# Two-layer diffusion backbone on one core: expert rows turned at the arm's end, results turned in pairs of units, arms at block heads

## The chip, the cores and the metric

One core of a Trainium2 chip runs the whole program. The metric is the device time of one execution in microseconds. The program uses the core's engines: TensorE (PE, matmuls and transposes), VectorE (DVE), ScalarE (ACT), GpSimd (POOL, here issuing DMAs and filling with zeros) and SyncE (SP, issuing the stream of weights). All data are float32; a float32 matmul is two matmul records in the trace, a transpose one.

## What is computed

A latent sequence of 256 tokens, width 1024, goes through two layers. Layer 0 is a mixer (attention and Fourier groups) and a dense SwiGLU. Layer 1 is a gated short convolution and then a mixture of experts, where the change is:

```python
def moe_swiglu(h, router, w_gate, w_up, w_down):
    probs = jax.nn.softmax((h @ router).astype(jnp.float32), axis=-1)
    vals, idx = lax.top_k(probs, TOP_K)                      # 2 of 8 experts per token
    wts = vals / jnp.sum(vals, axis=-1, keepdims=True)
    combine = jnp.sum(jax.nn.one_hot(idx, N_EXPERTS) * wts[..., None], axis=-2)
    out = jnp.zeros_like(h)
    for e in range(N_EXPERTS):
        out = out + combine[..., e:e + 1] * swiglu(h, w_gate[e], w_up[e], w_down[e])
    return out
```

Each expert has gate and up weights of 1024 x 3584 and down weights of 3584 x 1024, 44 MB together. Only the tokens that chose an expert are computed by it.

## The kernel before

**The stream of weights.** All weights lie in one tensor in the order of use and are read in units of 2 MB into a ring of seven slots (`ring`). SyncE issues them in this order (L254); each waits until TensorE has handed its slot back (`used`). An expert has 14 gate/up units (`GU_UNITS`) and 7 down units.

**Arms.** How many tokens an expert has is known only at run time. For each of seven widths (64, 96, 128, 144, 160, 192, 256 token rows) TensorE has a code of its own, an arm: L1341 and what follows, once per width. Behind each arm stands a chain of compare-and-branch instructions (`enter_arm`, L1199 to L1201) that jumps to the arm of the next expert. The other engines run one loop over the eight experts. In this run the widths are 64, 96, 144, 64, 128, 64, 96, 64.

**Gate and up.** In the narrow arms (64 and 96) the tokens' rows hTe are the stationary side and the ring's weights move (L1256); the product has tokens on the partitions. ScalarE takes the silu (L456), VectorE multiplies (L804) into aT. Since down needs channels on the partitions, the result of each unit is transposed: `turn` (L1226) is issued for unit u-1 behind the matmuls of unit u, into PSUM bank 6 or 7 by u's parity, and ScalarE's `take_turned` (L449) copies the whole bank of 512 columns back into aT. The last unit is turned inside the first down unit. For 32-row parts (in arm 96) two units share one transpose. In the wide arms (128 and up) the weights are the stationary side (L1238) and nothing has to be turned.

**Down and combine.** Seven down units (L1301) accumulate in banks 4 to 7; behind the last of them the result y is copied to SBUF, half by ScalarE (L475) and half by VectorE (L812), both waiting for `ye_ps`. `combine` (L1327) waits for both copies (`ye_act`, `ye_dve`), multiplies y by the weighted selection selT, and VectorE adds the four results to y_sum (L816). Combine's first matmul hands the last down unit's slot back.

**The next expert's rows.** The rows routed to each expert lie in DRAM; GpSimd reads the 1 MB of an expert into xn (L310) as soon as TensorE has transposed the expert before it (`gather_ps`). `turn_expert` (L1174) transposes xn into banks 0 to 3 in 16 transposes; it waits for xn and for all gate/up products of the present expert. `take_gather` modulates the result into hTe, four pieces of 128x256 on ScalarE (L435) and four on VectorE (L784). `turn_expert` is called in `down` behind unit `TURN_AFTER` = 3. On ScalarE and VectorE, `take_gather` stands between the expert's gate/up work and its copies of y.

An arm begins by waiting for hTe (`hTe_act`, `hTe_dve`).

Of the kernel before, what the change touches and what calls it, by code (L numbers as in the profile page):

```python
# [21 lines left out]
P = 128  # L22
# [22 lines left out]
PART = 256  # L45
WIDTHS = (64, 96, 128, 144, 160, 192, 256)
WIDE = 2
TURN_AFTER = 3


BLOCKS = {64: [(0, 64)], 96: [(0, 64), (64, 32)], 128: [(0, 128)], 144: [(0, 128), (128, 32)],
# [47 lines left out]
def build(nc, stream, x_in, ctx_in, vecs, consts, rope, dft, gains, ada_b, norm_w, late, out):  # L99
    ctx = ExitStack()  # L100
    with ctx:
# [213 lines left out]
        def _(act):  # L315
# [127 lines left out]
            with act.Fori(0, E) as e:  # L443
                act.reg_alu(which, widths, 7, ALU.bitwise_and)
                act.reg_alu(widths, widths, 3, ALU.logical_shift_right)

                def take_turned(u):
                    act.wait_ge(eT_ps, e * GU_UNITS + u + 1)
                    act.activation(aT_e[:, u, :, :].rearrange("p b n -> p (b n)"), ps[:, 6 + u % 2, :],  # L449
                                   ACT.Copy).then_inc(eT_ok, 1)  # L450

                def silu_units(wide):
                    for u in range(GU_UNITS):
                        act.wait_ge(e_ps, e * GU_UNITS + u + 1)
                        q = 2 * (u % 2)
                        act.activation(gated_e[:, u % 2, :, :], ps[:, q:q + 2, 0:SEQ], ACT.Silu).then_inc(e_silu, 1)  # L456
                        if u and not wide:
                            take_turned(u - 1)
                        if u == 5:
                            act.wait_ge(selT_ps, e + 1)  # L460
                            act.activation(selT[:, :, :].rearrange("p b t -> p (b t)"), ps[:, 4, :],
                                           ACT.Copy).then_inc(selT_ok, 1)
                    if wide:
                        act.sem_inc(eT_ok, GU_UNITS)
                    else:
                        take_turned(GU_UNITS - 1)

                with act.If_lt(which, WIDE):
                    silu_units(False)
                with act.Else():  # L470
                    silu_units(True)
                take_gather(e * 4 + 4)
                for b in (1, 0):
                    act.wait_ge(ye_ps, e * 4 + 4 - 2 * b)
                    act.activation(y_slot[:, b, 0:BANK], ps[:, 4 + 2 * b, :], ACT.Copy).then_inc(ye_act, 1)  # L475
# [353 lines left out]
        def _(pe):  # L829
# [365 lines left out]
            def enter_arm(name):  # L1195


                for i, width in enumerate(WIDTHS[:-1]):
                    pe.br_eq(which, i, on_true=f"arm{width}", on_false=f"{name}_not{width}")  # L1199
                    nc.switch_bb(f"{name}_not{width}")  # L1200
                pe.br(f"arm{WIDTHS[-1]}")  # L1201

            def is_wide(width):
                return WIDTHS.index(width) >= WIDE
# [9 lines left out]
                    return [] if u % 2 else [u - 2, u - 1] if u else []  # L1214
                return [u - 1] if u else []

            def turn(e, width, u):

                pe.wait_ge(e_a, e * GU_UNITS + u + 1)
                if u >= 2:  # L1220
                    pe.wait_ge(eT_ok, e * GU_UNITS + u - 1)
                for b, (s0, n) in enumerate(BLOCKS[width]):
                    if n == 32 and u % 2 == 0:
                        continue
                    for c in range(2 if n == P else 1):
                        last = pe.transpose(ps[:, 6 + u % 2, b * 256 + c * P:b * 256 + (c + 1) * P],  # L1226
                                            aT_e[:, u, b, c * P:(c + 1) * P], ident)
                last.then_inc(eT_ps, 1)

            def gate_up(e, width):  # L1230
                for u in range(GU_UNITS):
                    landed_of(e, u)
                    if u >= 2:
                        pe.wait_ge(e_a, e * GU_UNITS + u - 1)
                    done, count = done_before(width, u), 0
                    for b, g, k in wide_steps(width):
                        w = ring[:, (BASE + u) % RING, k * 512 + g * 256 + b * P:k * 512 + g * 256 + (b + 1) * P]
                        last = pe.matmul(ps[:, 2 * (u % 2) + b, g * SEQ:g * SEQ + width], w, hTe[:, k, 0:width],  # L1238
                                         start=(k == 0), stop=(k == KD - 1))
                        if count < len(done):  # L1240
                            last.then_inc(used[(BASE + done[count]) % RING], 1)
                        count += 1
                    for b, (s0, n) in enumerate([] if is_wide(width) else BLOCKS[width]):
                        tiles = P // n
                        if tiles == 4 and u % 2 == 0:
                            continue
                        bank = 2 * (u % 2) + b
                        for k in range(KD):
                            for r in range(tiles):
                                v = u if tiles < 4 else u - 1 + r // 2  # L1250
                                w = ring[:, (BASE + v) % RING, k * 512:(k + 1) * 512]
                                to = ps[n * r:n * (r + 1), bank, :]
                                if tiles > 1:
                                    w = w.rearrange("p (g c n) -> p g c n", g=2, c=2)[:, :, r % 2, :]
                                    to = to.rearrange("p (g c n) -> p g c n", g=2, c=2)[:, :, 0, :]
                                last = pe.matmul(to, hTe[:, k, s0:s0 + n], w, start=(k == 0), stop=(k == KD - 1))  # L1256
                                if count < len(done):
                                    last.then_inc(used[(BASE + done[count]) % RING], 1)
                                count += 1
                    last.then_inc(e_ps, 1)  # L1260
                    if u == 1:
                        pe.wait_ge(comb_ok, e * 4 + 4)
                    if u and not is_wide(width):
                        turn(e, width, u - 1)
                    if u == 5:

                        pe.wait_ge(selw_ok, e + 1)
                        for b, (s0, n) in enumerate(BLOCKS[width]):
                            for t in range(TB):
                                for r in range(P // n):  # L1270
                                    last = pe.matmul(ps[n * r:n * (r + 1), 4, b * SEQ + t * P:b * SEQ + (t + 1) * P],
                                                     selw[:, t, s0:s0 + n], ident, start=True, stop=True)
                        last.then_inc(selT_ps, 1)

            def down(e, width):
# [4 lines left out]
                for d in range(NFE // 4):  # L1280
# [5 lines left out]
                    for b, (s0, n) in (blocks[::-1] if d == final else blocks):  # L1286
# [22 lines left out]
                        if d < final and b == len(blocks) - 1:  # L1309
                            last.then_inc(used[s], 1)  # L1310
                        if d == 0 and b == 0 and not is_wide(width):
                            turn(e, width, GU_UNITS - 1)
                    if d == TURN_AFTER:
                        turn_expert(e)
                if is_wide(width):
# [135 lines left out]
```

## Time and profile before

| | us |
|---|---|
| median of 3 runs | 1543.69 (1540.67 to 1544.56) |
| profiled execution | 1544.38 |
| its span | 1542.5 |
| TensorE busy in it | 1462.2 (95%) |
| chain that ended last: TensorE, DMA, VectorE, issue | 84%, 9%, 4%, 2% |
| transposes of gate/up results (L1226) | 98 |
| ScalarE evictions of them (L449) | 84, 49.9 busy |
| transposes of the experts' rows (L1174) | 128 |

The expert part runs from 578.8 us to the end. TensorE is busy nearly throughout, but the experts of arm 64 end with TensorE waiting for landings of the ring. "Issue" in the chain is time in which an engine waited for nothing that the profile shows. Ends of matmuls are modelled. PEclk is the granted clock of TensorE, 1.00 for 2.4 GHz and 0.50 for 1.2 GHz.

### The profile page before, as it was taken

The numbers are of one execution on the slowest core, as the hardware profiler recorded it, in microseconds if no ns is written. First come the engines' busy times: TensorE is split into PE (matmuls) and PEld (weight loads), VectorE is DVE, ScalarE is ACT, GpSimd is POOL, SyncE is SP. The second block draws the span as 40 slices with busy tenths as digits, with TensorE's granted clock in tenths as the row PEclk, the third lists the DMA queues.
The fourth block names the chain that finished last, engine by engine and source line by source line (L and its number), as shares of the span: only waits on it lengthen the run. The fifth ranks groups of instructions, "written<-read, shape, count | busy, mean of one in ns | idle before, by whom it ended". The sixth has DMA issues, their size and how long they took to land.

```text
span 1542.5 us, 21924 instructions
## 1 busy us (share of the span) xinstructions
PE 1462.2 (95%) x9456; PEld 936.5 (61%) x9456; DVE 378.1 (25%) x658; ACT 257.9 (17%) x501; POOL 28.5 (2%) x32
## 2 busy tenths in 40 slices
PE   5999999999999969989989999998999999999897
PEld 2445498884488556445449984454997464553452
DVE  2659512330047432111010100111010111110112
ACT  3236210000110022211110000121010121121122
POOL 1000002000000001000000000000000000000000
PEclk8899999999999979999999999999999999999999
DMA  9864267971659539999987776799978899999895
GB/s 384 343 240 184 106 275 285 423 274 55 218 203 369 223 109 370 429 425 425 427 351 273 254 259 257 280 428 425 426 294 307 308 404 425 428 427 425 366 428 243
DMA packets 39023, 492.71 MB, mean 319 GB/s; under 512 B 4032, under 2 KB 4320, under 8 KB 10512
## 3 DMA queue, kind: packets, MB, share of 16 engines
q1 hardware_dynamic: 32800, 467.90, 75.1%
q0 software_dynamic: 5840, 22.26, 3.8%
q8 instruction: 88, 1.44, 0.4%
q10 hardware_dynamic: 288, 1.05, 0.2%
q14 instruction: 7, 0.06, 0.0%
HBM read 479.66 MB, written 11.53 MB: 318 GB/s over the span
## 4 chain that ended last, share of the span: by engine, by line
PE 84%; DMA 9%; DVE 4%; issue 2%; ACT 1%; SPq 0%; DVEq 0%
PE ps L1256 21%; PE ps L1301 15%; PE ps L1238 14%; PE ps L1040 10%; DMA ring<-stream 9%; PE ps L1017 9%; PE ps L1091 5%; PE ps L886 4%; PE ps L1226 1%; PE ps L1327 1%; DVE acc L547 1%; DVE att L610 1%; PE ps L1163 1%; PE ps L1174 1%; PE ps L988 0%
## 5 line engine op out<-in xcount | busy, mean ns | idle before, releaser
L1256 PE MATMUL ps<-ring,hTe 128*64 128x256 f32 (+1 forms) x3584 | 359.4, 382 | 7.6 <-issue 3.7
L1301 PE MATMUL ps<-ring,aT 128*64 128x512 f32 (+2 forms) x1232 | 287.0, 597 | 10.2 <-DMA ring<-stream 8.8
L1256 PEld LDWEIGHTS ps<-ring,hTe 128*64 128x64 f32 (+1 forms) x3584 | 215.2, 130 | 129.6 <-issue 16.9
L1238 PE MATMUL ps<-hTe,ring 128*128 128x144 f32 (+1 forms) x1792 | 214.7, 284 | 8.5 <-issue 8.5
L1238 PEld LDWEIGHTS ps<-hTe,ring 128*128 128x128 f32 x1792 | 214.0, 194 | 10.3 <-issue 10.3
L1301 PEld LDWEIGHTS ps<-ring,aT 128*64 128x64 f32 (+2 forms) x1232 | 96.9, 139 | 184.1 <-issue 174.8
L804 DVE TENSOR_TENSOR aT<-hT,ps 128x512 f32<-128x512 f32 x112 | 77.0, 688 | 526.1 <-ACT hT L456 526.1
L456 ACT ACTIVATE hT<-ps 128x512 f32<-128x512 f32 x112 | 66.9, 597 | 522.4 <-PE ps L1256 312.2
L1040 PE MATMUL ps<-hT,ring 128*128 128x256 f32 (+1 forms) x832 | 153.4, 347 | 0.0
L1040 PEld LDWEIGHTS ps<-hT,ring 128*128 128x128 f32 x832 | 138.1, 191 | 15.7 <-issue 1.0
L547 DVE SCALAR_TENSOR_TENSOR acc<-ring,silu_c,acc 128x1024 f32<-128x1024 f32 (+1 forms) x92 | 105.2, 1143 | 2.1 <-DVE acc L547 0.2
L1017 PE MATMUL ps<-ring,aT 128*128 128x512 f32 x240 | 104.5, 594 | 0.0
L1091 PE MATMUL ps<-hT,ring 128*128 128x256 f32 (+1 forms) x480 | 83.9, 337 | 0.0
L1091 PEld LDWEIGHTS ps<-hT,ring 128*128 128x128 f32 x480 | 76.2, 191 | 7.9 <-issue 0.5
L1017 PEld LDWEIGHTS ps<-ring,aT 128*128 128x128 f32 x240 | 45.1, 190 | 56.2 <-issue 56.2
L784 DVE TENSOR_SCALAR hTe<-ps,ab 128x256 f32<-128x256 f32 x36 | 17.2, 537 | 179.6 <-PE ps L1174 171.7
L449 ACT ACTIVATE aT<-ps 128x512 f32<-128x512 f32 x84 | 49.9, 594 | 18.2 <-PE ps L1226 18.2
L886 PE MATMUL ps<-ring,hT 128*128 128x512 f32 x96 | 43.1, 610 | 1.3 <-DVE hT L534 1.3
L435 ACT ACTIVATE hTe<-ps,ab 128x256 f32<-128x256 f32 x36 | 17.5, 563 | 154.9 <-PE ps L1174 145.7
L1226 PEld LDWEIGHTS ps<-cst,aT 128*128 128x128 f32 x98 | 12.5, 139 | 35.2 <-issue 35.2
L886 PEld LDWEIGHTS ps<-ring,hT 128*128 128x128 f32 x96 | 18.8, 197 | 24.7 <-issue 23.7
L812 DVE COPY acc<-ps 128x512 f32<-128x512 f32 x16 | 10.7, 689 | 84.5 <-PEq L1285 61.7
(190 smaller groups left out, 708.5 us busy)
## 6 DMA issues: line engine op xcount, KB each, us to landing
ring<-stream SPq DMA_DIRECT2D x222, 2048.0 KB, 13.5
rows_of_experts<-aT POOLq DMA_DIRECT2D x1, 8192.0 KB, 60.2
xn<-rows_of_experts POOLq DMA_DIRECT2D x8, 1024.0 KB, 17.0
gg<-norm_w POOLq DMA_DIRECT2D x4, 512.0 KB, 14.7
x<-x_in SPq DMA_DIRECT2D x1, 1024.0 KB, 5.1
hTe<-ctx_in SPq DMA_DIRECT2D x1, 1024.0 KB, 7.9
out<-x ACTq DMA_DIRECT2D x2, 512.0 KB, 2.7
aT<-dft POOLq DMA_DIRECT2D x1, 512.0 KB, 11.1
```

What stands on the lines that cost most here:

```text
L449: act.activation(aT_e[:, u, :, :].rearrange("p b n -> p (b n)"), ps[:, 6 + u % 2, :], ACT.Copy).then_inc(eT_ok, 1)
L456: act.activation(gated_e[:, u % 2, :, :], ps[:, q:q + 2, 0:SEQ], ACT.Silu).then_inc(e_silu, 1)
L547: last = dve.scalar_tensor_tensor(out=dst, in0=slot(what)[:, k * D:(k + 1) * D][:, cols], scalar=silu_c[:, 4 * h + k, 0:1], in1=dst, op0=A ...
L804: dve.tensor_tensor(aT_e[:, u, :, :], gated_e[:, u % 2, :, :], ps[:, q:q + 2, SEQ:2 * SEQ], ALU.mult).then_inc(e_a, 1)
L886: last = pe.matmul(ps[:, blk, :], lhs[:, k, b * P:(b + 1) * P], w[:, k, :], start=(k == 0), stop=(k == KD - 1))
L1017: last = pe.matmul(ps[:, 4 + 2 * b + h, :], lhs(k)[:, b * P:(b + 1) * P], w[:, k % per_unit, h * BANK:(h + 1) * BANK], start=(k == 0), sto ...
L1040: last = pe.matmul(ps[:, j % 4, g * SEQ + t0:g * SEQ + t1], w[:, j % 2, g, k, :], hT[:, k, t0:t1], start=(k == 0), stop=(k == KD - 1))
L1091: last = pe.matmul(ps[:, bank, c + t0:c + t1], w[:, i % 4, k, :], hT[:, k, t0:t1], start=(k == 0), stop=(k == KD - 1))
L1226: last = pe.transpose(ps[:, 6 + u % 2, b * 256 + c * P:b * 256 + (c + 1) * P], aT_e[:, u, b, c * P:(c + 1) * P], ident)
L1238: last = pe.matmul(ps[:, 2 * (u % 2) + b, g * SEQ:g * SEQ + width], w, hTe[:, k, 0:width], start=(k == 0), stop=(k == KD - 1))
L1256: last = pe.matmul(to, hTe[:, k, s0:s0 + n], w, start=(k == 0), stop=(k == KD - 1))
L1301: last = pe.matmul(ps[n * r:n * (r + 1), 4 + bank, :], a_T, w[:, f, half * BANK:(half + 1) * BANK], start=(j < max(1, tiles // 2)), stop=( ...
```

## The change

Three edits. `TURN_AFTER` goes from 3 to 6, the last down unit. `turn` takes a pair of units and is issued behind every even unit from 2 on, and once inside the first down unit; a pair's transposes lie in one bank, 128 columns for each unit and block, and one eviction takes them. Ahead of the last branch in each `enter_arm` stands an instruction that aligns addresses, so that the next arm begins at the head of a block of 256 instructions.

```diff
-TURN_AFTER = 3
+TURN_AFTER = NFE // 4 - 1
...
-                def take_turned(u):
-                    act.wait_ge(eT_ps, e * GU_UNITS + u + 1)
-                    act.activation(aT_e[:, u, :, :].rearrange("p b n -> p (b n)"), ps[:, 6 + u % 2, :],
-                                   ACT.Copy).then_inc(eT_ok, 1)
+                def take_turned(pair):
+                    act.wait_ge(eT_ps, e * GU_UNITS + 2 * pair + 2)
+                    act.activation(aT_e[:, 2 * pair:2 * pair + 2, :, 0:P],
+                                   ps[:, 6 + pair % 2, :].rearrange("p (u b n) -> p u b n", u=2, b=2),
+                                   ACT.Copy).then_inc(eT_ok, 2)
...
-                        if u and not wide:
-                            take_turned(u - 1)
+                        if u and u % 2 == 0 and not wide:
+                            take_turned(u // 2 - 1)
...
+                pe.addr_align(256, offset=255, max_nops=0)
                 pe.br(f"arm{WIDTHS[-1]}")
...
-            def turn(e, width, u):
+            def turn(e, width, pair):
 
-                pe.wait_ge(e_a, e * GU_UNITS + u + 1)
-                if u >= 2:
-                    pe.wait_ge(eT_ok, e * GU_UNITS + u - 1)
-                for b, (s0, n) in enumerate(BLOCKS[width]):
-                    if n == 32 and u % 2 == 0:
-                        continue
-                    for c in range(2 if n == P else 1):
-                        last = pe.transpose(ps[:, 6 + u % 2, b * 256 + c * P:b * 256 + (c + 1) * P],
-                                            aT_e[:, u, b, c * P:(c + 1) * P], ident)
-                last.then_inc(eT_ps, 1)
+                pe.wait_ge(e_a, e * GU_UNITS + 2 * pair + 2)
+                if pair >= 2:
+                    pe.wait_ge(eT_ok, e * GU_UNITS + 2 * pair - 2)
+                for u in range(2):
+                    for b, (s0, n) in enumerate(BLOCKS[width]):
+                        if n == 32 and u == 0:
+                            continue
+                        last = pe.transpose(ps[:, 6 + pair % 2, u * 256 + b * P:u * 256 + (b + 1) * P],
+                                            aT_e[:, 2 * pair + u, b, 0:P], ident)
+                last.then_inc(eT_ps, 2)
...
-                    if u and not is_wide(width):
-                        turn(e, width, u - 1)
+                    if u and u % 2 == 0 and not is_wide(width):
+                        turn(e, width, u // 2 - 1)
...
-                            turn(e, width, GU_UNITS - 1)
+                            turn(e, width, GU_UNITS // 2 - 1)
```

TensorE's order at the end of arm 64, from the first down unit to the chain of branches, before (L1226 turns the last unit, L1301 is down, L1174 the next expert's rows, L1327 combine; a count is that of matmuls in the program):

```order
L1301 MATMUL ps<-ring,aT 64x512 x8
L1219 REGISTER_ALU
L1226 MATMUL ps<-cst,aT 128x128
L1301 MATMUL ps<-ring,aT 64x512 x8
L1180 REGISTER_ALU
L1301 MATMUL ps<-ring,aT 64x512 x16
L1169 ISA
L1174 MATMUL ps<-cst,xn 128x128 x16
L1301 MATMUL ps<-ring,aT 64x512 x24
L1320 ISA
L1327 MATMUL ps<-acc 128x512 x4
```

and in the changed kernel, where the same lines are L1303, L1228, L1175 and L1329:

```order
L1303 MATMUL ps<-ring,aT 64x512 x8
L1221 REGISTER_ALU
L1228 MATMUL ps<-cst,aT 128x128 x2
L1303 MATMUL ps<-ring,aT 64x512 x8
L1181 REGISTER_ALU
L1303 MATMUL ps<-ring,aT 64x512 x40
L1170 ISA
L1175 MATMUL ps<-cst,xn 128x128 x16
L1322 ISA
L1329 MATMUL ps<-acc 128x512 x4
L1350 REGISTER_ALU
```

The 16 transposes of the next expert's rows now stand between the last down matmul and combine.

VectorE's order at the end of each expert, in the changed kernel (L785 modulates the gathered rows, L813 copies y, L817 adds the combined results); but for the line numbers the order is that of before:

```order
L785 TENSOR_SCALAR hTe<-ps,ab 128x256 x2
L784 REGISTER_ALU
L785 TENSOR_SCALAR hTe<-ps,ab 128x256 x2
L812 REGISTER_ALU
L813 COPY acc<-ps 128x512
L812 REGISTER_ALU
L813 COPY acc<-ps 128x512
L817 TENSOR_TENSOR acc<-acc,ps 128x512
```

Nothing moved on VectorE: its copies of y stand behind the modulated copies in both programs.

## Rows read from the trace of the kernel before

**Rows 1.** Chain that ended last, in order of time: start us, us, what

```profile
796.70 3.33 issue
...
1068.08 5.14 issue
1073.22 45.36 PE ps L1238 x384
...
1119.03 57.17 PE ps L1238 x512
...
1443.63 3.41 issue
```

**Rows 2.** Timeline, end of e3: start us, us, engine, line, operation, count [idle before <-releaser]

```profile
1051.39 1.97 PE L1174 MATMUL ps<-cst,xn 128*128 128x128 f32 x16
1052.08 1.93 ACT L435 ACTIVATE hTe<-ps,ab 128x256 f32<-128x256 f32 x4 [10.44 <-PE ps L1174]
1052.96 1.90 DVE L784 TENSOR_SCALAR hTe<-ps,ab 128x256 f32<-128x256 f32 x4 [14.69 <-PE ps L1174]
...
1053.28 7.09 PE L1301 MATMUL ps<-ring,aT 128*64 128x512 f32 x32
...
1061.73 1.29 DVE L812 COPY acc<-ps 128x512 f32<-128x512 f32 x2 [6.88 <-PEq L1285]
1061.76 3.65 PE L1301 MATMUL ps<-ring,aT 128*64 128x512 f32 x16 [1.38 <-DMA ring<-stream]
...
1066.10 1.99 PE L1327 MATMUL ps<-acc 64*128 64x512 f32 x8 [0.69 <-ACT acc L475]
```

**Rows 3.** Timeline of TensorE in e1 (arm 96), transposes between gate/up units

```profile
681.29 0.33 PE L1226 MATMUL ps<-cst,aT 128*128 128x128 f32 x1
681.55 3.67 PE L1256 MATMUL ps<-ring,hTe 128*64 128x256 f32 x32
685.16 0.44 PE L1226 MATMUL ps<-cst,aT 128*128 128x128 f32 x2
685.53 4.68 PE L1256 MATMUL ps<-ring,hTe 128*64 128x256 f32 x48
```

**Rows 4.** Timeline of TensorE from e0 to e1, then from e5 to e6

```profile
663.09 3.65 PE L1301 MATMUL ps<-ring,aT 128*64 128x512 f32 x16 [2.60 <-DMA ring<-stream]
...
669.35 3.67 PE L1256 MATMUL ps<-ring,hTe 128*64 128x256 f32 x32
674.10 7.26 PE L1256 MATMUL ps<-ring,hTe 128*64 128x256 f32 x96 [1.07 <-DMA ring<-stream]
...
1309.58 3.65 PE L1301 MATMUL ps<-ring,aT 128*64 128x512 f32 x16 [1.29 <-DMA ring<-stream]
...
1321.03 1.30 PE L1256 MATMUL ps<-ring,hTe 128*64 128x256 f32 x10 [1.52 <-DMA ring<-stream]
```

**Rows 5.** Stretches, while the next arm's code is due: us, engines, PEclk, DMA share, GB/s

```profile
1227.00:1229.50 2.50, 2.50 (x7) 1.06 (x7) 0.77 (x2) 1.00 (x1) 0.00 (x0) 1.00 0.40 85
1444.00:1446.00 2.00, 0.00 (x0) 0.00 (x0) 1.30 (x3) 0.00 (x0) 0.00 (x0) 1.00 0.99 410
```

**Rows 6.** Timeline of TensorE: near the start, from e4 to e5, head of e7

```profile
23.01 3.48 PE L864 MATMUL ps<-ring,silu_c 128*2 128x512 f32 x16 [2.94 <-DMA ring<-stream]
...
1226.71 3.70 PE L1327 MATMUL ps<-acc 128*128 128x512 f32 x8 [0.69 <-ACT acc L475]
1230.67 7.34 PE L1256 MATMUL ps<-ring,hTe 128*64 128x256 f32 x64 [0.27 <-issue]
...
1447.04 8.54 PE L1256 MATMUL ps<-ring,hTe 128*64 128x256 f32 x64 [3.41 <-issue]
```

**Rows 7.** Stretches behind three idle times; the columns of rows 5

```profile
23.00:26.00 3.00, 2.99 (x16) 0.44 (x16) 0.00 (x0) 0.00 (x0) 0.00 (x0) 0.53 1.00 425
661.00:665.00 4.00, 1.91 (x10) 0.92 (x12) 1.29 (x2) 0.60 (x1) 0.00 (x0) 1.00 1.03 432
...
1446.60:1449.90 3.30, 2.86 (x14) 1.76 (x16) 0.00 (x0) 0.00 (x0) 0.00 (x0) 0.50 0.73 313
```

More of the change, by code:

```diff
@@ L465, in silu_units @@
                     else:
-                        take_turned(GU_UNITS - 1)
+                        take_turned(GU_UNITS // 2 - 1)
                 with act.If_lt(which, WIDE):
```

## The prediction

> **What bounds the kernel now.** I read the chain that ended last first, in order of time [rows 1]. In the expert part (from 578.8 us on) it consists of TensorE matmuls, broken by landings of weight units and by three pieces called issue: 3.33, 5.14 and 3.41 us in which TensorE has no work between two experts. The eight experts need arms 64, 96, 144, 64, 128, 64, 96, 64; I call them e0 to e7. An arm-64 expert works through a gate/up unit in 3.87 us (3.61 in [rows 3] and 0.26 for a transpose), while a 2 MB unit at the 432 GB/s of [rows 7] takes 4.9 us: e0, e3 and e5 catch up with the stream and end waiting for it [rows 2, 4]. e1, e2, e4, e6 and e7 are bound by TensorE. A delay of an expert's start also delays the slots it hands back, so it passes on in full even through e3 and e5; only TensorE work inside the waiting stretch of e0, e3 and e5 is free.
>
> **1. The rows move behind the last down unit.** The 16 transposes take 1.89 us of TensorE wherever they stand (1051.39 to 1053.28 in [rows 2]). What hangs on them does not. ScalarE and VectorE execute in program order, and in both programs their four modulated copies of the gathered rows stand ahead of their copies of the down result; combine waits for the latter. Before, the modulated copies ran under the last three down units: ScalarE started 0.69 and VectorE 1.57 us after the transposes' start, VectorE was busy for 1.90 us, and nobody noticed. At the expert's end the down copies were ready, and combine began 0.69 us after the last down matmul (1065.41 to 1066.10).
>
> In the new place the same sequence starts at the last down matmul's end: VectorE begins at 1.57, is done at 3.47, then makes its two down copies, 1.29 us (1061.73 in [rows 2]), to 4.78; combine starts at about 4.8. ScalarE starts 0.9 earlier, also with four modulated and two down copies, and is not the last. So combine comes 4.8 instead of 0.7 after the last down matmul, 4.1 later, less the 1.9 that no longer stand between the units: **+2.2 us** where TensorE is the bound. For wide arms I take the same: there too combine began 0.69 after the last down matmul [rows 6], and VectorE's two copies, of which one used to lie under the last unit, now both come late. Five places are of this kind: e1 to e2, e2 to e3, e4 to e5, e6 to e7, and the end of e7, whose transposes serve nobody but are issued: 5 x 2.2 = 11.0.
>
> Behind a stream-bound expert the 1.9 are no gain, since they lay in its wait, but something else is: the 1 MB reload of xn that the transposes release moves out of the way of the last units. It costs the ring half a unit's time, 2.4 us, and I put half of that, 1.3, before the last down unit's landing and all of it before the landing of the next expert's second unit.
> - e3 to e4: 4.1 - 1.3 = 2.8, in round terms **+2.7**.
> - e0 to e1: last down starts 663.1 - 1.3, ends 3.65 later, combine 4.8 after that, the arm 1.9 after combine: 672.1; its second unit starts 3.6 later at 675.7 against 674.10 now, which was set by a landing [rows 4]: **+1.6**.
> - e5 to e6 likewise: 1309.6 - 1.3 + 3.65 + 4.8 + 1.9 + 3.6 = 1322.2 against 1321.03: **+1.2**.
>
> Together 16.5. The ring slot that combine's first matmul hands back also comes 4.1 later, but behind e2 and e4 the unit loaded into it is needed only six units on, and behind the others five or more slots are already queued: nothing.
>
> **2. Pairs.** In [rows 3] one transpose costs 0.26 us from its start to the next gate/up matmul, two in a row 0.37; so the first costs 0.26 and each further one 0.11. A pair of units cost 0.26 + 0.26 in arm 64 and costs 0.37; in arm 96 it cost 0.26 + 0.37 and costs 0.48: 0.15 less, seven times an expert, 1.05. Three narrow experts are bound by TensorE (e1, e6, e7): **-3.2**. In e0, e3 and e5 it vanishes in the wait for the stream. ScalarE saves seven of fourteen evictions, but it idles between units. The pair's later eviction holds nobody: the down units wait for theirs in the same order, and the last pair is turned inside the first down unit, as the last unit was.
>
> **3. Arms at block heads.** I take the three stalls as the fetch of the next arm's code, since TensorE waits there for nothing that the profile shows; from combine's start (1066.10 in [rows 2]) to the arm's (1073.22 in [rows 1]) it is 7.1 us. Would a block head shorten it? [rows 6] speaks against it: arm 64 was entered at the same instruction from e4 and from e6, once 3.96 us after combine's start with 0.27 of idle time, once with 3.41 idle. What differs is the load on the DMA engines that have to bring the code: share 0.40 behind e4, where no stall is seen, 0.99 behind e6, where one is [rows 5]. The code waits behind weight units, wherever in a block it starts. Between 0 and all three stalls (11.9 us) I take **0**.
>
> The Trainium skill, Runtime: NRT & Kernel Launch, section Instruction fetch mechanics, has it that a taken branch to a block outside the two that are present must wait for the fetch. It says nothing about the place within a block, and by it a jump into the next block, which arm 96 behind arm 64 now becomes, stays free: by the page this edit is worth 0.
>
> **4. TensorE's clock.** The move makes a new idle stretch of 4.8 - 1.9 = 2.9 us at each of eight ends. The idle stretch of 3.41 us ahead of e7 was followed by half clock, 1.2 GHz (0.50 granted in the 3.3 us from 1446.6), one of 2.94 near the start as well (0.53 in the 3 us behind it); one of 2.60, ended at 663.09, was not (1.00) [rows 4, 6, 7]. 2.9 lies between. The price: e4's first 384 matmuls took 45.36 us where 57.17/512 gives 42.9, 2.5 too many [rows 1]; e7's first 64 took 8.54 against e5's 7.34, 1.2 [rows 6]. Behind e1, e3 and e6 a slow combine hides in the wait for the code, and the arm's head ran at half clock already: nothing new. In the other five places (ends of e0, e2, e4, e5, e7) a fall costs about 1.5 us, as combine and the next matmuls run slow. Bounds 0 and 5 x 1.7 = 8.5; since the nearest row (2.94) fell and the next one below did not, I take three of five: **+4.5**.
>
> **Sum.** 16.5 - 3.2 + 0 + 4.5 = +17.8 on the profiled execution's 1544.4 us (span 1542.5 and 1.9 around it) is 1562.2; the median shown, 1543.7, is 0.7 lower: **1561.5 us**, 1.2% slower. With the clock term at its ends and 1 to 2 us of doubt in the stream-bound places, this case reaches from 1554 to 1568.
>
> **Rivals.**
> - *Block heads pay (the other side).* If the fetch of an arm that starts inside a block is what takes 7.1 us, because the little that is left of the block runs out and a second fetch is awaited, then all three stalls go (11.9), and with them the half clock behind them (2.5, 1.2, and 1.8 taken for e2, between them: 5.5): 13.3 - 17.4 = -4.1, 1539.6; each fall of the clock from term 4 adds 1.5. It wins as soon as the heads give more than the 13 to 18 us of the other terms. For it: the stalls are real and the largest idle pieces. Against it: [rows 5, 6]. 10%.
> - *The late jump finds the stream drained.* Combine now comes some 3 us later behind e1 and e6, and the transfers were near their end there: 0.73 share right behind e7's start [rows 7]. If the code is then fetched as fast as behind e4, each arm starts up to 3.3 us earlier and warm: 2 x (3.3 + 1.5) = 9.6 less, 1552. 9%.
> - *Arm 96 loses its free entry.* Behind arm 64 it followed directly in the program and was entered without a stall (at 669.35 in [rows 4], where its combine had just ended). Now padding lies between, and its block may have to be fetched: 7.1 - 1.9 = 5.2 us twice, and half clock behind each: about 1573. 8%.
> - Something else, such as copies that overlap more than I assume: 3%.
>
> **How the numbers follow.** The forecast's case has 70%. The range leaves out the first rival and the upper half of the third: 1549 to 1571. A measurement of this kernel can tell about 0.3%, 4.6 us, from no change. The first rival lies at that bound, 1540 with no fall of the clock and up to 1546 with some: I split it with half of the rest into faster 5% and same 7%; everything else is slower, 88%.
>
> **What would show it.** Right: the modulated copies directly behind the last down matmul, with TensorE idle for 2.9 us before combine at all eight ends; 7 instead of 14 evictions in narrow experts with gaps of 0.37 per pair; the three stalls still of 3 to 5 us under a full DMA load. Wrong: combine within 2 us of the transposes' end; arm starts less than 5 us after combine behind e1, e3 and e6 (first or second rival, told apart by the DMA share there); an issue gap ahead of e1 and e6 (third). Clock: no granted 0.5 behind e0, e2, e4 and e5 takes 4.5 off.

## The result

The changed kernel takes 1557.72 us (median of 4 runs, 1557.08 to 1559.65) against 1543.4 for the kernel before (1540.67 to 1544.56): ratio 1.0097, 95% interval 1.008 to 1.0115. That is 14.3 us slower, where 17.8 were forecast, and inside the range. Its profiled execution took 1557.08, span 1555.2.

Line numbers in the changed kernel are 1 or 2 higher: L1258 and L1240 gate/up, L1303 down, L1175 the rows' transposes, L435 and L785 the modulated copies, L476 and L813 the y copies, L1329 combine. First the page's group of combine (busy us, mean ns, then idle time of TensorE ahead of it and who ended it):

```profile
L1329 PE MATMUL ps<-acc 64*128 64x512 f32 (+1 forms) x88 | 33.0, 814 | 22.8 <-DVE acc L813 22.8
```

TensorE stands idle for 22.8 us ahead of combine, eight times 2.84, and each time VectorE's y copy ends it. The timeline of the changed kernel at the end of e3, which answers to [rows 2] (start us, us, engine, line, operation, count, idle before and its releaser):

```profile
1062.86 3.65 PE L1303 MATMUL ps<-ring,aT 128*64 128x512 f32 x16 [1.33 <-DMA ring<-stream]
1066.44 1.97 PE L1175 MATMUL ps<-cst,xn 128*128 128x128 f32 x16
1067.14 1.93 ACT L435 ACTIVATE hTe<-ps,ab 128x256 f32<-128x256 f32 x4 [24.56 <-PE ps L1175]
1068.01 1.90 DVE L785 TENSOR_SCALAR hTe<-ps,ab 128x256 f32<-128x256 f32 x4 [28.57 <-PE ps L1175]
1068.71 0.71 POOL L310 DMA_DIRECT2D xn<-rows_of_experts  x1 [90.11 <-PE ps L1175]
1068.95 1.09 ACT L476 ACTIVATE acc<-ps 128x512 f32<-128x512 f32 x2
1069.83 1.28 DVE L813 COPY acc<-ps 128x512 f32<-128x512 f32 x2
...
1071.25 3.42 PE L1329 MATMUL ps<-acc 64*128 64x512 f32 x8 [2.84 <-DVE acc L813]
1073.38 2.60 DVE L817 TENSOR_TENSOR acc<-acc,ps 128x512 f32<-128x512 f32 x4 [2.27 <-PE ps L1329]
1078.11 2.28 PE L1240 MATMUL ps<-hTe,ring 128*128 128x128 f32 x9 [3.44 <-issue]
```

The last down matmul ends at 1066.51, VectorE's last copy at 1071.11, combine starts at 1071.25: 4.74 instead of 0.69 us behind the last down matmul.

Over the expert part the two profiled traces differ by 13.3 us. Where they went, expert by expert, from the first gate/up matmul of one to that of the next (of e7: to the end of its combine), worked out from the TensorE timelines. The last two columns are pieces of it; "wait" is from the last down matmul to combine, "jump" from combine's start to the next arm's first matmul:

| | period before | after | difference | wait before, after | jump before, after |
|---|---|---|---|---|---|
| e0 | 90.5 | 94.3 | +3.8 | 0.69, 4.74 | 1.92, 2.48 |
| e1 | 130.7 | 129.9 | -0.8 | 0.70, 4.74 | 7.04, 5.33 |
| e2 | 182.9 | 183.5 | +0.5 | 0.69, 4.59 | 5.55, 5.52 |
| e3 | 90.2 | 92.2 | +1.9 | 0.69, 4.74 | 7.12, 6.86 |
| e4 | 157.5 | 159.7 | +2.3 | 0.69, 4.59 | 3.97, 4.95 |
| e5 | 85.2 | 88.9 | +3.7 | 0.69, 4.74 | 1.92, 3.58 |
| e6 | 131.2 | 130.2 | -1.0 | 0.70, 4.74 | 7.12, 6.70 |
| e7 | 84.9 | 87.8 | +2.8 | 0.70, 4.74 | - |

The wait grew everywhere by the same 3.9 to 4.05. The rest differs from place to place, and that is where the forecast was off.

### The profile page after: what moved, and what is told of

Its sections match the earlier page's. It is cut to its first block, busy times and chain, and to the rows that moved or that the text cites. A ratio compares the mean times of both kernels' runs of the same rounds, so it can differ in the third digit from the quotient of the medians.

```text
span 1555.2 us, 21842 instructions
## 1 busy us (share of the span) xinstructions
PE 1457.1 (94%) x9456; PEld 935.9 (60%) x9456; DVE 377.4 (24%) x658; ACT 236.0 (15%) x459; POOL 28.5 (2%) x32
## 3 DMA queue, kind: packets, MB, share of 16 engines
q10 hardware_dynamic: 288, 1.05, 0.2%
## 4 chain that ended last, share of the span: by engine, by line
PE 82%; DMA 10%; DVE 5%; issue 2%; ACT 1%; SPq 0%; DVEq 0%; ACTq 0%
PE ps L1258 21%; PE ps L1240 14%; PE ps L1303 13%; DMA ring<-stream 10%; PE ps L1041 10%; PE ps L1018 8%; PE ps L1092 5%; PE ps L887 4%; PE ps L1329 2%; DVE acc L548 1%; DVE att L611 1%; PE ps L1228 1%; PE ps L1175 1%; DVE hTe L785 1%; PE ps L1164 1%
## 5 line engine op out<-in xcount | busy, mean ns | idle before, releaser
L1258 PE MATMUL ps<-ring,hTe 128*64 128x256 f32 (+1 forms) x3584 | 353.3, 382 | 3.1 <-issue 1.3
L1303 PE MATMUL ps<-ring,aT 128*64 128x512 f32 (+2 forms) x1232 | 287.5, 597 | 20.0 <-DMA ring<-stream 17.2
L1258 PEld LDWEIGHTS ps<-ring,hTe 128*64 128x64 f32 (+1 forms) x3584 | 216.9, 130 | 130.5 <-issue 25.1
L1303 PEld LDWEIGHTS ps<-ring,aT 128*64 128x64 f32 (+2 forms) x1232 | 97.3, 139 | 201.5 <-issue 176.9
L1240 PE MATMUL ps<-hTe,ring 128*128 128x144 f32 (+1 forms) x1792 | 212.1, 282 | 3.4 <-issue 3.4
L1240 PEld LDWEIGHTS ps<-hTe,ring 128*128 128x128 f32 x1792 | 211.4, 192 | 5.6 <-issue 5.6
L785 DVE TENSOR_SCALAR hTe<-ps,ab 128x256 f32<-128x256 f32 x36 | 17.2, 537 | 317.6 <-PE ps L1175 309.5
L435 ACT ACTIVATE hTe<-ps,ab 128x256 f32<-128x256 f32 x36 | 17.5, 562 | 292.6 <-PE ps L1175 283.2
L1329 PE MATMUL ps<-acc 64*128 64x512 f32 (+1 forms) x88 | 33.0, 814 | 22.8 <-DVE acc L813 22.8
L1329 PEld LDWEIGHTS ps<-acc 64*128 64x128 f32 (+1 forms) x88 | 12.7, 245 | 36.3 <-issue 36.3
L681 DVE TENSOR_TENSOR aT<-hTe,ps 128x256 f32<-128x256 f32 x22 | 9.2, 420 | 88.0 <-ACT hTe L418 88.0
```

Of the source, the lines that this page charges most:

```text
L785: dve.tensor_scalar(hTe[:, k, :], ps[:, k // 2, (k % 2) * SEQ:(k % 2 + 1) * SEQ], ab[:, 4, 0, k:k + 1], ab[:, 4, 1, k:k + 1], ALU.mult, AL ...
L1303: last = pe.matmul(ps[n * r:n * (r + 1), 4 + bank, :], a_T, w[:, f, half * BANK:(half + 1) * BANK], start=(j < max(1, tiles // 2)), stop=( ...
L1329: last = pe.matmul(ps[:, 4 + i, :], selT[rows, b, t * P:(t + 1) * P], y_slot[rows, b, y0:y0 + BANK], start=(b == 0), stop=(b == len(blocks ...
```

## The experiments

The theory: the move costs, because the modulated copies stand ahead of the y copies in two in-order queues; pairs give a little, block heads nothing; the stalls ahead of e2, e4 and e7 are the fetch of code behind weight units. Each run is timed against the kernel before on the same chip, which took 1543.43, 1542.96 and 1543.92 us there; so a difference between two variants is good to about 1 us. Each variant has one trace; where its execution was not a typical one, that is said.

### One part at a time

**The move undone.** On the changed kernel:

```diff
-TURN_AFTER = NFE // 4 - 1
+TURN_AFTER = 3
```

> The changed kernel with the rows' transposes back behind down unit 3; pairs and block heads stay. My theory (the move alone costs, pairs give 3.2 us in the three TensorE-bound narrow experts, heads give nothing): 1540 us, 0.2% under the kernel before, combine again 0.7 us after the last down matmul, and stalls of 3 to 5 us ahead of e2, e4 and e7. Rival (heads remove the stalls): 1525 to 1530. Rival (pairs or heads carry the loss): above 1550.

Measured: 1542.34 us, ratio 0.999 (0.998 to 1.0001). Combine 0.69 to 0.70 behind the last down matmul, stalls of 3.58, 5.35 and 3.45 us ahead of e2, e4 and e7. The move carries the whole loss. Pairs and heads together are worth about 1 by the medians, with an interval that just includes no gain; 1540 and 3.2 were expected. The trace is of the fastest of twelve executions (1538.42), 3.9 below the median, so only parts of it are used. e7 took 82.19 us from its first matmul to its last down matmul against 82.25 before, because an idle time of 1.31 us ahead of a down unit (at 1519.71 in its trace) has come in where the kernel before had none. e7 had been just ahead of the stream, and is not any more.

**The move alone.** On the kernel before:

```diff
-TURN_AFTER = 3
+TURN_AFTER = NFE // 4 - 1
```

> The kernel before with TURN_AFTER = 6 and nothing else. My theory: combine 4.8 us after the last down matmul at all eight ends, 1558 to 1561 us, that is the changed kernel's time and up to 3 more for the lost pairs. Rival (the change's loss sits in heads or pairs): 1544.

Measured: 1561.22 us, ratio 1.0106 (1.0093 to 1.012): +17.8 us. Combine 4.74 (narrow) and 4.59 (wide) behind the last down matmul at all eight ends. The changed kernel is 3.5 below it, near the 3.2 of the pairs; pairs and heads together are thus worth 3.5 with the move and 1.1 without it. The arms of e2, e4 and e7 began 5.08, 7.02 and 5.01 us behind combine, with 1.37, 4.13 and 1.31 us of idle time: two of the three stalls of the kernel before are 2 us shorter here, by the move alone.

**Block heads alone.** On the kernel before:

```diff
+                pe.addr_align(256, offset=255, max_nops=0)
                 pe.br(f"arm{WIDTHS[-1]}")
```

> The kernel before with the aligned arms and nothing else. My theory (the code waits behind weight units, wherever it starts): 1543 us within 1.5, the three stalls as before, combine start to arm start 7.1 us. Rival (an entry inside a block is what costs): the three stalls and the half clock behind them gone, 1526. Rival (arm 96 loses its free entry behind arm 64): 5 us more idle ahead of e1 and e6, 1550 or more.

Measured: 1543.72 us, ratio 0.9994 (0.9983 to 1.0005). Stalls of 3.71, 5.27 and 3.29 us, jumps of 7.4, 7.25 and 7.0 us, and arm 96 starts 1.92 behind arm 64's combine as before. Both rivals on the heads fall: no help and no cost can be seen, the interval reaching from 2.6 us less to 0.8 more.

### What in the move costs

**The y copies first.** On the changed kernel, for ScalarE (VectorE alike):

```diff
-                take_gather(e * 4 + 4)
                 for b in (1, 0):
                     act.wait_ge(ye_ps, e * 4 + 4 - 2 * b)
                     act.activation(y_slot[:, b, 0:BANK], ps[:, 4 + 2 * b, :], ACT.Copy).then_inc(ye_act, 1)
+                take_gather(e * 4 + 4)
```

> The changed kernel, but ScalarE and VectorE copy y before they modulate the gathered rows. My theory (the loss is those modulated copies ahead of the y copies): combine about 2 us after the last down matmul, directly behind the transposes, no idle 2.8 us and no fall of the clock from it, 1535 to 1541 us. Rival (the transposes' new place costs by itself, whatever the order of the copies): 1555 to 1558.

Measured: 1535.23 us, ratio 0.9937 (0.9926 to 0.9949), 22.5 below the changed kernel and 8.2 below the one before. Its timeline at the end of e3:

```profile
1057.80 0.60 ACT L475 ACTIVATE acc<-ps 128x512 f32<-128x512 f32 x1 [20.74 <-PEq L1287]
1057.80 1.29 DVE L812 COPY acc<-ps 128x512 f32<-128x512 f32 x2 [23.87 <-PEq L1287]
1057.82 3.65 PE L1303 MATMUL ps<-ring,aT 128*64 128x512 f32 x16 [1.34 <-DMA ring<-stream]
1061.40 1.97 PE L1175 MATMUL ps<-cst,xn 128*128 128x128 f32 x16
1061.51 0.60 ACT L475 ACTIVATE acc<-ps 128x512 f32<-128x512 f32 x1 [3.12 <-PE ps L1303]
...
1062.97 1.90 DVE L785 TENSOR_SCALAR hTe<-ps,ab 128x256 f32<-128x256 f32 x4 [3.89 <-PE ps L1175]
1063.30 1.99 PE L1329 MATMUL ps<-acc 64*128 64x512 f32 x8
```

The y copies run under the last down unit and the transposes, and combine follows the transposes without a gap, 1.83 us behind the last down matmul (1.58 in wide arms). Now the new place is better than the old: it covers the 0.69 that TensorE used to wait. The rival, that the place itself costs, falls.

**Only VectorE's y copies first.** The same edit on VectorE alone.

> The changed kernel with only VectorE's y copies ahead of its modulated copies; ScalarE keeps its order. My theory (4.8 us is VectorE's queue; ScalarE's is 0.69 + 1.93 + 2 x 0.60 + the way to TensorE = 3.9): combine 3.9 us after the last down matmul instead of 4.74, TensorE idle for about 2.0 instead of 2.8 at each end, 1548 to 1552 us. Rival (VectorE's order is all that matters): combine at 1.8.

Measured: 1553.94 us in one run; combine 3.58 behind the last down matmul (3.43 in wide arms), released by ScalarE. So VectorE was the later of two queues that both expose the work; taking it away moves the wait to the other. 3.9 was 0.3 too high, 0.1 of it because ScalarE's two copies take 1.09 together and not 1.20. The time missed the 1548 to 1552: the eight waits gave back 9.3 us over the trace, but the experts' part fell by only 3.5. The earlier combine met longer waits for the next arm's code (arms of e2, e4, e5 and e7 7.07, 7.25, 6.06 and 6.75 us behind combine, 5.33, 6.86, 4.95 and 6.70 in the changed kernel), and e2's head ran slow again (175.01 us from its first matmul to its last down matmul against 173.33).

**One unit earlier.** On the changed kernel:

```diff
-TURN_AFTER = NFE // 4 - 1
+TURN_AFTER = NFE // 4 - 2
```

> The changed kernel with the rows' transposes one unit earlier, behind down unit 5. VectorE needs 3.47 us from the transposes' start to the end of its modulated copies, and the last down unit of arm 64 lasts 3.6. My theory (only work that outlasts the last unit is exposed): combine 0.7 to 0.8 us after the last down matmul, no fall of the clock from it, 1539 to 1542 us. Rival (the loss comes from the transposes or the xn reload meeting the end of the expert): 1550 or more.

Measured: 1539.49 us, ratio 0.9975 (0.9965 to 0.9985). Its timeline at the end of e3:

```profile
1056.30 1.97 PE L1175 MATMUL ps<-cst,xn 128*128 128x128 f32 x16
...
1057.87 1.90 DVE L785 TENSOR_SCALAR hTe<-ps,ab 128x256 f32<-128x256 f32 x4 [23.57 <-PE ps L1175]
1058.20 3.65 PE L1303 MATMUL ps<-ring,aT 128*64 128x512 f32 x16
...
1059.69 1.28 DVE L813 COPY acc<-ps 128x512 f32<-128x512 f32 x2
1061.90 0.60 ACT L476 ACTIVATE acc<-ps 128x512 f32<-128x512 f32 x1 [2.48 <-PE ps L1303]
1062.55 1.99 PE L1329 MATMUL ps<-acc 64*128 64x512 f32 x8 [0.70 <-ACT acc L476]
```

One down unit of 3.65 us covers the modulated copies: combine starts 0.70 behind the last down matmul again, and the run is 18.2 us below the changed kernel.

**The copies first on the kernel before**, with the move, without pairs and heads.

> The kernel before with the transposes behind the last down unit and the y copies ahead of the modulated copies; no pairs, no block heads. My theory (the parts add up): 3 to 4 us above the version with pairs and heads (1535.2), so 1537 to 1539. Rival (the gain under the kernel before comes from pairs and heads together): 1543.

Measured: 1537.65 us, ratio 0.9963 (0.9951 to 0.9974), 2.4 above the version with pairs and heads, between the 1.1 and the 3.5 that these were worth above. 5.3 us of the gain are there without them, and the 0.69 us that no longer stand ahead of combine at eight ends make 5.5.

### The stalls ahead of the arms

**Half of each transfer left out.** On the kernel before, SyncE's loop; the experts' part gets a loop of its own, in which a transfer brings half of its unit, so the products are not those of the kernel and only the times count:

```diff
-                    sp.dma_start(ring[:, s, :], stream[lap * RING + s, :, :]).then_inc(landed[s], 16)
+                    sp.dma_start(ring[:, s, 0:UNIT // 2],
+                                 stream[lap * RING + s, :, 0:UNIT // 2]).then_inc(landed[s], 16)
```

> The kernel before, but from the experts' part on each ring transfer brings only the first half of its unit, so that the DMA engines are idle about half of the time; the products use stale second halves, the work of the engines is the same. My theory (the code of the next arm waits behind weight units): ahead of e2, e4 and e7 combine start to arm start falls from 7.1 us to 4 to 4.6, so the idle stretch falls to under 1 us behind arm 96 and to 2 to 2.6 behind arm 64 (a shorter combine). Rival (the jump itself takes 7 us): 3.3, 5.1 and 3.4 us of idle time as before.

Measured: 1521.02 us in one run. Jumps behind e1, e3 and e6 of 4.79, 4.14 and 4.01 us instead of 7.04, 7.12 and 7.12. From e6 to e7 in its timeline (L1332 is combine, L1261 gate/up), and two stretches from combine's start to the next arm, behind e1 and behind e6 (us, busy of PE, PEld, DVE, ACT, POOL, granted clock, DMA share, GB/s):

```profile
1420.97 3.70 PE L1332 MATMUL ps<-acc 64*128 64x512 f32 x16 [0.70 <-ACT acc L480]
1424.98 5.40 PE L1261 MATMUL ps<-ring,hTe 128*64 128x256 f32 x48 [0.31 <-issue]
```

```profile
786.00:791.00 5.00, 3.70 (x16) 1.46 (x16) 1.84 (x4) 1.50 (x2) 0.00 (x0) 1.00 0.50 147
1421.00:1425.00 4.00, 3.69 (x18) 1.46 (x18) 1.14 (x2) 1.25 (x1) 0.00 (x0) 1.00 0.46 123
```

With the DMA engines half idle the stalls of 3.33, 5.14 and 3.41 us become 1.09, 2.16 and 0.31, the arms and their places unchanged. The load is the cause of 2.3 to 3.1 of the 7 us; the jump itself takes some 4, which combine of arm 96 (3.7) nearly covers and that of arm 64 (2.0) does not.

**Arms at slot 200.** On the kernel before:

```diff
+                pe.addr_align(256, offset=199, max_nops=0)
                 pe.br(f"arm{WIDTHS[-1]}")
```

> The kernel before with every arm beginning at slot 200 of a block of 256, so that 56 instructions (some 3 us) are left in the block that the jump fetches. My theory has the second block fetched under the same load: if it is asked for only when the jump has landed, a second stall of 1 to 3 us some 3 us into e2, e4 and e7, 1545 to 1552 us. Rival (the place in the block never matters): no such stall, 1543. Rival (a block head is what helps, mid-block costs): more than 1555.

Measured: 1551.57 us, ratio 1.0049 (1.003 to 1.0069). The head of e7 in its timeline (L1328 combine, L1257 gate/up):

```profile
1452.87 3.23 PE L1257 MATMUL ps<-ring,hTe 128*64 128x256 f32 x26 [3.35 <-issue]
1458.37 3.89 PE L1257 MATMUL ps<-ring,hTe 128*64 128x256 f32 x34 [2.27 <-issue]
```

A second stall 3.2 us into the arm, 2.27 us; likewise 2.07 in e2, 1.20 in e3, 0.72 in e4 and 2.30 in e5, behind every jump, where I had expected it in e2, e4 and e7. Together 8.6, as much as the run lost. e4's first 26 matmuls ran partly at half clock and took 4.68 us instead of 3.23, so less of the fetch was left to wait for. The place in the block does matter when so little of it is left. The kernel before has no stall of this kind behind a jump; that its arms leave enough of their first block, so that heads had nothing to give, is my reading of it.

### The reload of xn

**A late reload.** On the changed kernel, GpSimd:

```diff
                 pool.wait_ge(gather_ps, 4 * (e + 1))
+                if e:
+                    pool.wait_ge(e_ps, e * GU_UNITS + 3)
```

> The changed kernel, but GpSimd reloads xn only when the next expert's third gate/up unit is multiplied, three to four units behind the jump. My theory (the code of the next arm waits behind whatever is queued; the 1.28 us stall ahead of e5, new in the changed kernel, is the reload's): behind e4 combine start to arm start falls from 4.95 back to about 4.0; the rest as in the changed kernel, 1554 to 1558 us. Rival (that stall comes from the block head or the longer jump): 4.95 stays.

Measured: 1564.6 us, ratio 1.0129 (1.0112 to 1.0145), 6.9 above the changed kernel: a miss in time. The arm of e5 did not start earlier either, as combine ran at half clock there (5.11 us) and covered the jump (5.04), whatever its length.

The records of the DMA packets settle the question all the same. On q8, the instruction queue, a packet of 16 KB starts shortly ahead of each of these arms; that it is the arm's code I take from its time. q1 is the stream of weights, and q0 carries the reload of xn in packets of 4 KB, one row each. DMA activity in 40 slices and queues (packets, MB, share), first in the kernel before in the 2 us from combine's start behind e4 (1226.71 to 1228.71), then in the changed kernel from 1232.90 to 1234.90 and from 1234.90 to 1236.50, then with the late reload from 1238.76 to 1240.76:

```profile
DMA  0000000000000000000000009000000000000000
q8 instruction: 1, 0.02, 2.9%
...
q0 software_dynamic: 205, 0.84, 101.8%
...
q8 instruction: 1, 0.02, 3.9%
...
DMA  0000000000000000000000000900000000000000
q8 instruction: 1, 0.02, 4.3%
```

In the kernel before the packet stands alone, 1.2 us behind combine's start. In the changed kernel the reload has the engines for the first 2 us, and the packet starts at 2.2. With the reload taken away it is back at 1.3. Start of the packet and of the next arm, in us behind combine's start:

| | e1 to e2 | e3 to e4 | e4 to e5 | e6 to e7 |
|---|---|---|---|---|
| before | 4.2, 7.0 | 4.2, 7.1 | 1.2, 4.0 | 4.3, 7.1 |
| changed | 2.2, 5.3* | 4.0, 6.9 | 2.2, 5.0 | 2.2, 6.7* |
| move alone | 2.2, 5.1 | 4.1, 7.0 | 2.1, 4.9 | 2.3, 5.0 |
| late reload | 1.7, 5.3* | 4.2, 7.0 | 1.3, 5.0* | 1.4, 5.1* |
| VectorE's copies first | 4.2, 7.1 | 4.4, 7.3 | 3.3, 6.1 | 3.9, 6.8 |
| y copies first | 4.6, 7.4 | 2.9, 5.7 | 0.3, 3.5* | 4.1, 6.9 |
| half of each transfer | 1.7, 4.8 | 1.4, 4.1 | 1.2, 4.3 | 1.3, 4.0 |

A star marks an arm that began with combine's end, the code being there. Everywhere else the first matmul came 2.7 to 3.1 us behind the packet's start. So the length of a jump is set by when the packet gets its turn.

The run also shows the price of the reload. It now falls into the stretch in which e3, e5 and e7 race with the stream, and their time from first matmul to last down matmul grew from 80.56, 80.58 and 81.02 to 83.01, 83.11 and 83.01 us: 2.4, 2.5 and 2.0. This agrees with the prediction's 2.4 for 1 MB, and makes it likely that getting the reload out of this stretch is a gain of the move.

**The same with the y copies first.**

> The y copies first, and the xn reload delayed as in the run with the late reload. My theory: behind wide experts the fetch of the code was already hidden, behind e1, e3 and e6 it waits for the ring's units and not for the reload; so little is left to gain, 1533 to 1536 us against 1535.2. Rival (the reload holds the code everywhere): arm starts 4 to 4.5 us after combine behind e1, e3 and e6, under 1530.

Measured: 1541.22 us, ratio 0.9982 (0.9972 to 0.9992), 6.0 above the version with the copies first alone, where 1533 to 1536 were expected: a miss, as the reload costs in e3, e5 and e7 (83.0, 82.9 and 83.3 us against 81.0, 81.3 and 82.3, together 4.5). The trace is of an execution 2.8 below the median and does not show the rest. Jumps behind e1, e3 and e6 took 6.9, 5.7 and 6.6 (with the copies first alone 7.4, 5.7 and 6.9): the reload is not what holds the code there, as expected.

## Why the prediction was right, and where it was off

The direction, the mechanism and its size held. The time was 3.8 us lower than forecast, within the forecast case's own 1554 to 1568.

1. **The move.** "Combine starts at about 4.8" was 4.74 (4.59 in wide arms, where the last matmuls end later in the model). The run with the copies first shows the cause, and the two that change only the place or one queue show the arithmetic. It also gives the price of the order alone: combine 4.74 instead of 1.83 us behind the last down matmul, 2.9 at each end, 22.5 in all. The sum of 16.5 for it alone, with 4.5 for the clock, was 21.0; the move alone measured 17.8.

2. **Stream-bound experts.** From first matmul to last down matmul e3 and e5 became 1.9 and 2.0 shorter; I had put 1.3, half of the reload. Whether half or nearly all of it had lain ahead of the last down unit, two traces can't tell: with the transposes in the old place e3 took 82.43, 81.76 and 81.00 us (before, move undone, heads alone), in the new one 80.5 to 81.0 in five runs (changed, move alone, VectorE's copies first, the y copies first on either kernel); e5 took 82.6 to 83.4, and 80.6 to 82.2. On average that is 1.0 and 1.5. And I had e7 among the experts bound by TensorE, though it has the arm whose pace I had found faster than the stream. In the changed kernel it is bound by the stream:

```profile
1524.48 3.65 PE L1303 MATMUL ps<-ring,aT 128*64 128x512 f32 x16 [1.15 <-DMA ring<-stream]
1529.37 3.65 PE L1303 MATMUL ps<-ring,aT 128*64 128x512 f32 x16 [1.24 <-DMA ring<-stream]
1534.32 3.65 PE L1303 MATMUL ps<-ring,aT 128*64 128x512 f32 x16 [1.30 <-DMA ring<-stream]
1537.90 1.96 PE L1175 MATMUL ps<-cst,xn 128*128 128x128 f32 x16
1542.71 1.99 PE L1329 MATMUL ps<-acc 64*128 64x512 f32 x8 [2.84 <-DVE acc L813]
```

From its first matmul to its last down matmul e7 took 81.02 us. With half of each transfer left out every expert of arm 64 took 80.8, which is TensorE's own pace; less 1.05 for the pairs and 1.9 for the transposes, 77.9 would be left. The three waits for landings above, 3.7 us, take 3.1 of this. e7's part came out at +2.8 instead of 2.2 - 1.05 = +1.15, although its head no longer ran slow. The trace of before hid this: e7 took 82.25 there, 80.8 and a slow head, and an expert that needs its units just when they land shows no wait.

3. **Pairs.** -3.2 forecast; 1.1 and 3.5 measured, together with the heads. That the ring swallows part of it is seen in e7; how much elsewhere was not measured. In the TensorE-bound e1 the run with the move undone gained 0.96 of the 1.05.

4. **Block heads.** 0 forecast, +0.3 us measured, which is none within its interval. The reason given, the load on the DMA engines, is shown by the halved stream and by the packets.

5. **The clock and the waits for code, the step that failed.** Forecast: three falls in five places, +4.5, and nothing new at the other three, where the wait for the code was to stay 7.1 us and the next arm's head slow. The idle stretch was 2.84 us at all eight ends, and the clock fell behind five of them (e0, e1, e3, e5, e6). In the places that I had priced it fell at two, e0 and e5, where jump took 2.48 and 3.58 instead of 1.92. But behind e1 and e6 the code came 2 us earlier than before, and with the stall went the slow head. TensorE from e1 to e2 and from e6 to e7 in the changed kernel, and stretches while code was due (the same columns as above):

```profile
797.17 5.40 PE L1329 MATMUL ps<-acc 64*128 64x512 f32 x16 [2.84 <-DVE acc L813]
802.51 9.70 PE L1240 MATMUL ps<-hTe,ring 128*128 128x144 f32 x77
...
1450.25 6.77 PE L1329 MATMUL ps<-acc 64*128 64x512 f32 x16 [2.84 <-DVE acc L813]
1456.95 10.58 PE L1258 MATMUL ps<-ring,hTe 128*64 128x256 f32 x96
```

```profile
798.50:801.00 2.50, 2.50 (x8) 1.22 (x6) 0.00 (x0) 0.00 (x0) 0.00 (x0) 0.50 0.96 275
1452.00:1453.50 1.50, 1.50 (x6) 0.73 (x4) 0.00 (x0) 0.00 (x0) 0.00 (x0) 0.50 0.62 202
1075.00:1077.00 2.00, 0.00 (x0) 0.00 (x0) 0.97 (x2) 0.00 (x0) 0.00 (x0) 1.00 1.02 418
```

Combine ran at half clock, 5.40 and 6.77 instead of 3.70 us, but under it the code arrived, and no idle time stood ahead of e2 and e7. Their heads ran at full clock: e7's first 96 matmuls in 10.58 us, where [rows 6] has 8.54 for 64, and e2's first 384 in 47.24 against 48.97 before. It is not the fall under combine that saved the heads: with the move alone combine ran at full clock at these two places, the stalls were 1.37 and 1.31, the heads ran at full clock too, and the arms began 5.08 and 5.01 us behind combine. The fall cost 0.3 and 1.7 of that.

This is the second rival, to which I had given 9%: the later jump met a stream that was through. Queues in the 2 us from combine's start in the changed kernel, behind e1 and behind e3:

```profile
q0 software_dynamic: 189, 0.77, 98.3%
q1 hardware_dynamic: 3, 0.00, 0.1%
...
q1 hardware_dynamic: 52, 0.79, 92.3%
```

Behind e1 (and e6, with 0.79 MB on q0) only the reload was under way, and the code's packet started at 2.2 us; behind e3 it was the stream, the packet started at 4.0, and the stall of 3.44 stayed. The DMA share, by which I had wanted to tell the rivals apart, showed this poorly, as the reload kept the engines busy. So it was not a matter of either case, but of place by place: the rival came true at two of three jumps, and a smaller loss of the same kind, the reload ahead of the code, came in at e4.

Against the kernel before, jumps behind e1, e3 and e6 gave back 1.71, 0.26 and 0.42 us, and the heads of e2 and e4 1.73 and 0.85: 4.97. (e7's head gave back 1.48, which its stream took; it is in item 2.) The new costs at e0, e5 and e4 were 0.56, 1.66 and 0.98, and e1's head ran slow for 1.1: 4.3. Clock and jumps together thus came to -0.7 us instead of +4.5.

6. **Sum.** 16.5 - 3.2 = 13.3 without clock and jumps; with -0.7 for these, -1.3 for the shorter e3 and e5, and +1.65 for e7, 12.95. The traces differ by 13.3 over the experts and by -0.6 ahead of them. The remainder of this sum is no better than 1 us, as the places share effects. That the forecast missed by only 3.8 is in part luck: 5.2 too much for clock and jumps and 1.3 too much for e3 and e5 stand against 1.65 too little for e7.

The Trainium skill (Runtime: NRT & Kernel Launch, Instruction fetch mechanics) has it that a taken branch out of the blocks that are present waits for a fetch. The runs agree: the entry into arm 96 behind arm 64 stays free at its own block head (1.92 us with heads alone), and a jump far off waits for a packet of 16 KB.

**Left open.** What decides whether the clock falls behind 2.84 us of idle time: it did at five of eight ends here and at four, in part others, with the move alone. And why, with the y copies first, the packet behind e3 started at 2.9 us and not at 4: with the reload delayed as well it was 2.9 again, so it is not the reload.

## What to carry to other kernels

Before a producer is moved later, list what stands behind its consumers in every in-order queue, not only what waits for it: here 16 transposes cost the same anywhere, and the modulated copies behind them held combine up by 2.9 us at each of eight ends until the order was swapped on both engines. The same move with the y copies first is the best version found, 1535.2 us, 0.6% under the kernel before. An engine that never waits for a stream may be just level with it; compare its pace with that of a sister stage that does wait, before counting a saving there. And a jump that comes later meets other transfers: look at what the queues hold in the 2 us behind it.

## What the hardware did that I had not expected

- A jump to code that is not there takes 4.0 to 4.8 us from combine's start with the DMA engines half idle and about 7.1 with 99% share: the packet of 16 KB with the instructions starts 1.2 to 1.7 us behind combine's start in the one case and 4.2 to 4.3 in the other, and the first matmul follows 2.7 to 3.1 us behind it.
- With 56 instructions left in the block that a jump lands in, TensorE stalls a second time, for 0.7 to 2.3 us.
- The same idle stretch of 2.84 us was followed by half clock at five of eight places in the changed kernel (e0, e1, e3, e5, e6) and at four (e2, e3, e5, e7) in the move alone. An idle stretch of 3.58 us in the run with the move undone (ahead of e2) was not followed by it (granted 1.00 from 798.5 to 802), and with only VectorE's copies first the clock was 0.50 from 1238.5 to 1241.5, behind idle stretches of 1.69 and 2.36 us.
